# A SwiGLU block's down projection in Strassen form: evictions, refill pieces and row transfers moved to other steps

## The reference, cut to what matters

```python
h = _rms_norm(x, norm_ffn[l])
g = h @ w_gate[l].astype(h.dtype)
u = h @ w_up[l].astype(h.dtype)
x = x + (jax.nn.silu(g) * u) @ w_down[l].astype(h.dtype)
```

## Time and profile before

| | us |
|---|---|
| median of 3 runs | 2599.43 (2596.59 to 2600.51) |
| the profiled execution's own time | 2598.14 |
| its span, first to last instruction | 2596.4 |
| PE busy | 2463.3 (95% of the span) |
| DVE, ACT, POOL busy | 1414.1, 1165.6, 1311.5 |
| mean granted TensorE clock | 0.984 of full speed |

### The profile page before, as it was taken

The page is one execution under the profiler, slowest core; times in us unless marked ns, Lnnn a source line. Parts: engine busy times, 40 slices in busy tenths (PEclk is TensorE's granted clock), DMA queues, the critical chain, the costliest instruction groups (busy, mean ns, idle before and its releaser), DMA issues.

```text
span 2596.4 us, 34828 instructions
## 1 busy us (share of the span) xinstructions
PE 2463.3 (95%) x12008; PEld 2032.5 (78%) x12008; DVE 1414.1 (54%) x1463; ACT 1165.6 (45%) x1864; POOL 1311.5 (51%) x916
## 2 busy tenths in 40 slices
PE   8899999999899999799979999999999999999999
PEld 6777877777777777678768888888777888888887
DVE  4333366776676666533665555553645555553343
ACT  3222267676677676432343333324443333332433
POOL 1454366767667677300465445422785544551243
PEclk9999999999999999899989999999999999999999
DMA  5988863443443432254323332348663233224766
GB/s 178 302 264 279 258 182 100 135 107 94 128 107 97 143 90 68 75 173 138 146 89 113 112 119 75 109 170 294 206 205 126 73 109 121 87 99 159 228 216 203
DMA packets 337225, 388.17 MB, mean 150 GB/s; under 512 B 21440, under 2 KB 242752, under 8 KB 334784
## 3 DMA queue, kind: packets, MB, share of 16 engines
q1 hardware_dynamic: 337088, 386.49, 46.9%
HBM read 263.20 MB, written 123.21 MB: 149 GB/s over the span
## 4 chain that ended last, share of the span: by engine, by line
PE 44%; POOL 3%; DMA 1%; DVE 1%; issue 1%; ACT 0%; SPq 0%; DVEq 0%; POOLq 0%; ACTq 0%
PE ffn_ps L2184 10%; PE ffn_ps L2186 10%; PE ffn_ps L2188 10%; PE ffn_ps L2214 4%; PE ffn_ps L2216 4%; PE ffn_ps L2215 4%; POOL ffn_A L2103 1%; DMA ffn_raw<-in_w_up 1%; POOL ffn_A L2108 1%; POOL all_B L2130 0%; DMA ffn_A_over<-in_w_down 0%; ACT ffn_A L1796 0%; DMA ffn_A_over<-x 0%; POOL ffn_s L2114 0%; DVE ffn_A L1975 0%
## 5 line engine op out<-in xcount | busy, mean ns | idle before, releaser
L2103 POOL TENSOR_TENSOR ffn_A<-ffn_raw,ffn_A 128x512 fp32r<-128x512 f32 x264 | 366.1, 1399 | 381.3 <-ACT ffn_A L1754 381.3
L2184 PE MATMUL ffn_ps<-all_B,ffn_A 128*128 128x512 f32 x1232 | 482.1, 391 | 17.8 <-POOL ffn_A L2103 15.3
L2186 PE MATMUL ffn_ps<-all_B,ffn_A 128*128 128x512 f32 x1232 | 481.5, 391 | 0.0
L2188 PE MATMUL ffn_ps<-all_B,ffn_A 128*128 128x512 f32 x1232 | 481.3, 391 | 0.0
L1059 DVE TENSOR_TENSOR_SCAN lay_stick<-lay_ps,lay_stick 128x128 f32<-128x128 f32 (+5 forms) x192 | 331.2, 1726 | 199.5 <-ACT lay_ps L963 189.6
L1110 POOL TENSOR_TENSOR lay_a<-lay_a,lay_stick 128x128 f32<-128x128 f32 (+5 forms) x192 | 281.4, 1472 | 219.9 <-DVE lay_stick L1059 219.1
L1754 ACT ACTIVATE ffn_A<-ffn_raw 128x512 fp32r<-128x512 f32 x264 | 162.2, 626 | 291.0 <-DMA ffn_raw<-in_w_gate 122.8
L2184 PEld LDWEIGHTS ffn_ps<-all_B,ffn_A 128*128 128x128 f32 x1232 | 232.5, 189 | 67.5 <-POOL ffn_A L2103 19.0
L1796 ACT ACTIVATE ffn_A<-ffn_A_over 128x1024 fp32r<-128x1024 f32 x154 | 163.1, 1060 | 253.0 <-PE ffn_ps L2216 227.7
L1975 DVE TENSOR_TENSOR ffn_A<-ffn_A_over,ffn_A 128x1024 fp32r<-128x1024 f32 x104 | 154.5, 1489 | 212.9 <-ACT ffn_A L1796 212.9
L2188 PEld LDWEIGHTS ffn_ps<-all_B,ffn_A 128*128 128x128 f32 x1232 | 232.4, 189 | 48.3
(11 more groups left out here) (135 smaller groups left out, 5036.0 us busy)
## 6 DMA issues: line engine op xcount, KB each, us to landing
hid_ops<-ffn_s SPq DMA_DIRECT2D x154, 256.0 KB, 2.0
ffn_A_over<-hid_ops SPq DMA_DIRECT2D x154, 256.0 KB, 3.0
lay_w_stage<-in_w_in SPq DMA_DIRECT2D x48, 512.0 KB, 4.2
ffn_raw<-in_w_gate SPq DMA_DIRECT2D x22, 1024.0 KB, 5.4
ffn_raw<-in_w_up SPq DMA_DIRECT2D x22, 1024.0 KB, 7.6
ffn_A_over<-wd_ops SPq DMA_DIRECT2D x88, 256.0 KB, 3.5
ffn_A_over<-in_w_down SPq DMA_DIRECT2D x66, 256.0 KB, 3.9
lay_wd_raw<-in_w_down SPq DMA_DIRECT2D x11, 1024.0 KB, 8.5
```

The lines of the kernel that those rows point to most:

```text
L2103: nc.gpsimd.tensor_tensor(A[:, j, p, 1, :, :], operand(j, p), A[:, j, p, 0, :, :].bitcast(F32), ALU.subtract).then_inc(lo_done, 1)
L2184: nc.tensor.matmul(ps[:, b, :], A[:, j, p, 0, k, :], B[p][:, 0, k, :], start=first_mm, stop=False, skip_group_check=True)
L2186: nc.tensor.matmul(ps[:, b, :], A[:, j, p, 0, k, :], B[p][:, 1, k, :], start=False, stop=False, skip_group_check=True)
L2188: mm = nc.tensor.matmul(ps[:, b, :], A[:, j, p, 1, k, :], B[p][:, 0, k, :], start=False, stop=last_mm, skip_group_check=True)
```

## The change

On DVE the evictions after D2, D7 and D4 are spread, one bank a step behind the step's low part (steps 24 to 27, 46 to 49, 58 to 61), where before all four stood in one step ahead of it (24, 46, 57). Those after D6 and D5 stay. The refill begins earlier: two `load_b` a step in steps 10 to 17 (one a step in 10 to 25), combinations from step 20 (26), high parts from 25 (31), low parts from 29 (34), a little farther apart. `y_to_21` begins at step 50 (51). `store_z` 0 and 1 stand at steps 34 and 67 (31 and 64), `load_z` 1 and 3 at 36 and 69 (34 and 67); `load_z` 2 stays at 53. The raw places are given to other products' tiles, so that round 11's `hi` of products 2 to 5 wait for single low parts. That of product 2 is issued ahead of the last `split`, and those of products 8 to 13 between the round's `keep`s; round 12's first two come behind them.

```diff
--- before.py
+++ after.py
@@ -1494,7 +1494,7 @@
 SUMS = [(GATE, P5), (GATE, P7), (UP, P5), (UP, P7), (GATE, P6), (UP, P6), (GATE, P3), (UP, P3)]
 C11, C12, C22, C21 = range(4)
 D1, D2, D6, D7, D4, D5, D3 = range(7)
-T_AT, B_HI_AT, B_LO_AT = 26, 31, 34
+T_AT, B_HI_AT, B_LO_AT = 20, 25, 29
 
 
 def ffn_stage(nc, cst, B, Bf, offset, x2_dram, h2_dram, ops_dram, wt_dram, w_gate, w_up, w_down, out):
@@ -1560,14 +1560,15 @@
 
             return of[:, j, p, :, :, :].rearrange("p h k c -> p (h k c)")
 
-        op_raw = [flat(Af, j, p) for j, p in ((GATE, P5), (GATE, P6), (UP, P5), (UP, P6))]
+        op_raw = [flat(Af, j, p) for j, p in ((UP, P6), (GATE, P5), (GATE, P6), (UP, P5))]
         hi_of = [flat(A, j, p) for j, p in ((GATE, P7), (UP, P7), (UP, P2))]
         lo_of = [flat(A, j, p) for j, p in ((GATE, P2), (GATE, P4), (UP, P4))]
         hid_part, wd_part = slice(0, BANK), slice(BANK, 2 * BANK)
         SETS = ((6, 7, 2, 3), (0, 1, 4, 5))
         set_of = {D1: 0, D2: 0, D6: 1, D7: 1, D4: 0, D5: 1, D3: 1}
 
-        hi_at, lo_at = ([first + 7 * m // 5 for m in range(28)] for first in (B_HI_AT, B_LO_AT))
+        hi_at, lo_at = ([first + 10 * m // 7 for m in range(28)] for first in (B_HI_AT, B_LO_AT))
+        t_at = [T_AT + 4 * m // 3 for m in range(16)]
 
         def z_pair(i):
 
@@ -1631,7 +1632,7 @@
             def load_op(G, e):
                 R, (d, c) = last_round(G), divmod(e, ROUNDS)
                 if e < RAWS:
-                    sp.wait_ge(prod_done, NP * R + 1 + (spot[GATE, P5], spot[GATE, P6], spot[UP, P5], spot[UP, P6])[e])
+                    sp.wait_ge(prod_done, NP * R + 1 + (spot[UP, P6], spot[GATE, P5], spot[GATE, P6], spot[UP, P5])[e])
                 else:
                     wait_lo(sp, G, e - RAWS)
                 if e == 0:
@@ -1716,17 +1717,18 @@
                     load_op(G, e)
                     if e == 9:
                         load_z(G, 0)
-                    if G == 0 and e - 10 in range(4 * GT):
-                        load_b(e - 10)
-                    if e == ENDS[D2] + 10:
+                    if G == 0 and e - 10 in range(2 * GT):
+                        load_b(2 * (e - 10))
+                        load_b(2 * (e - 10) + 1)
+                    if e == ENDS[D2] + 13:
                         store_z(G, 0)
-                    if e == ENDS[D2] + 13:
+                    if e == ENDS[D2] + 15:
                         load_z(G, 1)
                     if e == 53:
                         load_z(G, 2)
-                    if e == ENDS[D4] + 10:
+                    if e == ENDS[D4] + 13:
                         store_z(G, 1)
-                    if e == ENDS[D4] + 13:
+                    if e == ENDS[D4] + 15:
                         load_z(G, 3)
                 store_z(G, 2)
                 store_w(G)
@@ -1745,8 +1747,11 @@
                 if R and R % ROUNDS == 0:
                     G = R // ROUNDS
                     if p in (P5, P6):
-                        act.wait_ge(dve_lo, ON_DVE * G)
-                        act.wait_ge(pool_lo, ON_POOL * G)
+                        wait_lo(act, G - 1, STEPS - RAWS + ((GATE, P5), (GATE, P6), (UP, P5), (UP, P6)).index((j, p)))
+                    elif (j, p) in ((UP, P2), (UP, P4)):
+                        act.wait_ge(tile_done, GT * (STEPS * G - 2))
+                    elif (j, p) in ((GATE, P7), (GATE, P2)):
+                        act.wait_ge(tile_done, GT * (STEPS * G - 1))
                     elif p in (P7, P2, P4):
                         act.wait_ge(tile_done, GT * STEPS * G)
                     elif p == P3:
@@ -1864,10 +1869,20 @@
                     more = R + 1 < HALVES * ROUNDS
                     ahead = more and not last
                     keep(R, GATE, 0)
+                    if c == 0:
+                        hi(R, 8)
+                        hi(R, 9)
                     keep(R, UP, 0)
-                    if more:
+                    if c == 0:
+                        hi(R, 10)
+                        hi(R, 11)
+                    if more and c:
                         hi(R + 1, 0)
                     keep(R, GATE, 1)
+                    if c == 0:
+                        hi(R, 12)
+                        hi(R, 13)
+                        hi(R + 1, 0)
                     if more:
                         hi(R + 1, 1)
                     if ahead:
@@ -1906,8 +1921,10 @@
                     split(G, e)
                     if G == 0 and e in hi_at:
                         b_hi_piece(hi_at.index(e))
+                    if e == STEPS - 2 and G + 1 < HALVES:
+                        hi(ROUNDS * (G + 1), 2)
                 if G + 1 < HALVES:
-                    for n in range(2, NP):
+                    for n in range(3, 8):
                         hi(ROUNDS * (G + 1), n)
 
         @block.vector
@@ -2081,14 +2098,17 @@
                     hidden(R, 3)
                     sums_of_hidden(R)
                 for e in range(OPS, STEPS):
-                    for d, evict in ((D2, evict_11), (D6, evict_w), (D7, evict_y), (D4, evict_21), (D5, evict_22)):
+                    for d, evict in ((D6, evict_w), (D5, evict_22)):
                         if e == ENDS[d] + OPS:
                             for t in range(GT):
                                 evict(G, t)
                     if e % 3 < 2:
                         op_lo(G, e)
-                    if G == 0 and e - T_AT in range(16):
-                        t_piece(e - T_AT)
+                    for d, evict, after in ((D2, evict_11, 3), (D7, evict_y, 3), (D4, evict_21, 4)):
+                        if e - ENDS[d] - after in range(GT):
+                            evict(G, e - ENDS[d] - after)
+                    if G == 0 and e in t_at:
+                        t_piece(t_at.index(e))
                 for t in range(GT):
                     evict_12(G, t)
                 if G + 1 < HALVES:
@@ -2142,7 +2162,7 @@
                 for e in range(STEPS):
                     if e % 3 == 2:
                         op_lo(G, e)
-                    for at, add in ((39, x2_to_w), (51, y_to_21), (ENDS[D5] + 4, y_to_22)):
+                    for at, add in ((39, x2_to_w), (50, y_to_21), (ENDS[D5] + 4, y_to_22)):
                         if e - at in range(0, 2 * GT, 2):
                             add(G, (e - at) // 2)
                     if G == 0 and e in lo_at:
```

## The result

| | before | after |
|---|---|---|
| median us (4 runs each) | 2598.01 (2596.51 to 2600.51) | 2616.72 (2614.34 to 2618.87) |
| profiled execution, us | 2598.14 | 2618.87 |
| span, us; mean granted clock | 2596.4; 0.984 | 2617.1; 0.982 |

The ratio is 1.0071, with a 95% interval of 1.0053 to 1.0088: the change makes the kernel 0.7% slower. PE's work is the same; what grew is the time in which it waits, and the time at the lower clock behind the waits.

A forecast was written before the change was run, and what follows sets the result against it. PE was taken as the bound, with some 13 us to gain from a better order of the first half. The terms summed to +13.3 on 2598.1, giving 2611 us, range 2600 to 2618.

The forecast's parts named there:

- crowded transfers: Rival: transfers of steps 10 to 17 become a bound, PE stalls repeatedly with a slow clock; 2617 us, chance 0.12.
- step 33: First half, at `evict_w`: one more POOL piece in the way of DVE, +1.1 us (0 to 1.3).
- step 11 (loads of B crowded): Steps 10 to 17: two blocks of B a step leave a lag, `keep_x` behind a late `split`; +0.5 us (0 to 3).
- steps 42 and 44: First half: two DVE combinations and one POOL piece less, waits shrink; -3.5 us (-4.2 to -2.5).
- step 53: First half: POOL's low part late behind the addition waiting for z, two pieces and a second addition; +4.7 us (1 to 7).
- steps 56 and 57: First half: additions done earlier and `evict_21` begins at 58, so both waits and their slow clock go; -3.8 us.
- step 66, first half: `evict_22` waits for the later fourth load of z, itself held by the store; +5.0 us, with the clock +6.6.
- round 11: The 2.49 wait goes, but round 12's weights load later: 2.5 idle at product 8, 1.5 at 9; +1.5 us (0 to 2.5).
- step 66, second half: Same late load of z, as SP's queue is one code for both halves; +4.6 us, with the clock +6.2.
- The clock: Behind a long wait PE runs at the lower clock, costing 1.6 us; a wait soon after another costs 1.2 to 1.6.
- the clock would hold: Rival: no slow clock behind the long waits and step 53 on time; 2602 us, chance 0.18.
- the load of z is hidden: Rival: the fourth load of z lands before DVE reaches `evict_22`, and step 53 is on time; 2594 us, chance 0.07.

The follow-up runs named there:

- experiment 6: Changed kernel with the refill's high and low parts back at steps 31 and 34, old spacing; combinations and loads stay early: 2612.55 us, ratio 1.0052.
- experiment 7: Changed kernel with the four `evict_w` moved ahead of step 34's combination: 2613.72 us, ratio 1.0057.
- experiment 3: Changed kernel with `y_to_21` beginning at step 51 again, as before: 2614.09 us, ratio 1.0058.
- experiment 4: On top of experiment 1, the third load of z at SP's step 50 instead of 53: 2596.10 us, ratio 0.9993.
- experiment 1: Changed kernel with the second store and fourth load of z back at SP's steps 64 and 67: 2603.83 us, ratio 1.0017.
- experiment 2: Kernel before with only the second store and fourth load of z moved to SP's steps 67 and 69: 2611.89 us, ratio 1.0053.
- experiment 8: On top of experiment 1, `keep` of products 5 and 8 ahead of round 12's `hi`: 2600.88 us, ratio 1.0009.
- experiment 5: Changed kernel with the refill's whole schedule (loads, combinations, high and low parts) back as before: 2610.45 us, ratio 1.0041.

## Why the prediction was right, and where its sizes were off

It said 2611 (2600 to 2618), slower; measured is 2616.7. The direction and the largest mechanism were right, and the sum is 5 to 6 short of it. That the time lies within the range is partly luck: the sum itself was expected at 2606 to 2614, and the range went up to 2618 for crowded transfers, which cost 0.8 here. What fills that room is above all step 33. Idle time and slow stretches by place, after minus before:

| place | predicted | measured |
|---|---|---|
| step 11 (loads of B crowded) | +0.5 | +0.8 |
| step 33 | +1.1 | +6.4 |
| steps 42 and 44 | -3.5 | -4.3 |
| step 53 | +4.7 | +6.9 |
| steps 56 and 57 | -3.8 | -4.0 |
| step 66, first half | +6.6 | +7.2 |
| round 11 | +1.5 | 0.0 |
| step 66, second half | +6.2 | +6.5 |
| sum | +13.3 | +19.5 |

The sum is 0.6 above the 18.9 that the profiled execution is longer by from step 0 on: the slow stretches are counted from starts of matmuls, and each is good to some tenths.

*Step 33* is the term that failed. "That puts one more piece in the way: +1.1 (0 to 1.3)" counted one of POOL's instructions and one turn. The order of DVE's list is unchanged there, as it said. But it left out the three pieces of steps 29 to 31. From the first of them on seven of the eight DVE instructions ahead of `evict_w`, all on two SBUF operands, take 1.8 to 2.9 us where they take 0.7 or 1.2 alone, and by the time of step 34's combination POOL's low part of step 35 has begun: another whole 2.44. Experiments 6 and 7 show both parts: without the early pieces 1.05, without that combination ahead 2.23 for 4.97. A wait of 5 us then also pays the clock, 2.5 here, which a wait of 1.04 had not.

By the Trainium skill, SBUF — State Buffer, section SBUF: two separate sides, DVE and POOL share a pair of ports to SBUF under an exclusive lock, which a DVE instruction with two inputs in SBUF needs as well. The rows of step 33 agree: a combination of 2.83 beside a POOL instruction of 2.44, and of 0.68 where POOL is idle. The four evictions, which read one operand from PSUM, take 2.47 beside POOL as before, as the prediction took from the page.

*Steps 42, 44, 56, 57:* right in place and within 0.8 of size. The reason given for 44 was half wrong: by experiment 6 it is POOL's pieces at their new steps, and the two combinations fewer on DVE do little there. With the additions back at 51 (experiment 3) 0.85 is at step 56 and nothing at 57, which speaks for the moved `evict_21` at 57; it was not tried alone.

*Step 53:* the mechanism was right (experiments 3 and 4). PE arrives there later than assumed, by the wait at step 33, and so does SP's load, by about as much (2.9 and 2.7 us after step 0). The idle time came out at 4.66 and the slow stretch at 2.3, for 3.1 and 1.6: from z to the low part's end it took 9.4, for the 8.5 of the prediction's working, and from the load's issue to the first addition 7.8 for 7.1.

*Step 66:* the size of the idle time was right to within 0.8: 5.05 for 5.8 (5.0 and the 0.80 of before) and 5.60 for 5.0 (4.6 and the 0.44). Experiments 1 and 2 show the mechanism from both sides. But one term of its working was too large: it let the store land 6.7 after its issue, so that it held the load of z by 1.3 in the first half and by 0.5 in the second. The store took 5.3 and 6.0, and the load follows step 69's loads at once. The load's second transfer in turn took 7.3 and 7.9 instead of the 7.0 assumed. These errors have opposite signs, and over the two halves they cancelled, which is luck. The cause is the load's two places later in SP's queue; in experiment 3 the store's landing adds 1.0 to it.

The Trainium skill's fit that the prediction sets beside this (DMA: Bandwidth & Descriptors, Anatomy of one DMA) is given there for transfers that GpSimd issues, and here SP does. By it the waits would have been some 3 us shorter; they were not.

*Round 11:* the mechanism was right (experiment 8), the size not. The second weights came 6.5 after their issue, not the 7.7 taken from the earlier trace rows, so the waits are 1.23 and 1.25. Timeline of SP and ACT, after:

```profile
1986.50 0.38 SPq L1617 DMA_DIRECT2D ffn_raw<-in_w_up  x1
1993.02 0.63 ACT L1759 ACTIVATE ffn_A<-ffn_raw 128x512 fp32r<-128x512 f32 x1 [2.06 <-DMA ffn_raw<-in_w_up]
1994.08 0.58 ACT L1779 ACTIVATE ffn_s<-ffn_ps 128x512 f32<-128x512 f32 x1
```

*The clock:* 1.6 behind a long wait was too little. It was 2.3 and 2.9 in the first half and 1.3 in the second, 6.5 for 4.8 over the three places where it was forecast, beside the 2.5 at step 33 that was not.

*The rivals:* that the clock would hold is excluded, 0.50 behind each of the first half's three long waits; that the load of z is hidden is excluded by DVE's idle 4.17 and 5.07 until its landing; the crowded transfers cost 0.84, at one place (at most 1.3 there in the other kernels that keep them). The spread evictions were not tried alone. Nor was it tried what moving the first store and second load of z (34 and 36) does by itself; no wait stands there.

## What to carry to other kernels

Find for each transfer the instruction that waits for it, and compare the time from its issue to that with the longest landing in the trace, not the median: two places later in a full queue cost 13 us here, because one order is run in both halves. Where DVE and POOL both read their operands from SBUF, a short instruction ahead of an eviction can cost as much as POOL's longest one, so what frees a PSUM bank belongs ahead of all that may have to take a turn. Before a small difference is explained, look at the stretches that the change cannot touch: here step 0 begins at 1731.3 to 1740.0 in the eleven profiled executions, 8.7 us apart, though PE's work ahead of it is the same in all.

## What the runs showed of the hardware that was not expected

The granted clock after a wait does not follow from its length, nor from a smaller wait ahead of it. A wait of 1.80 at step 57 was followed by a slow stretch in the kernel before, and the same one, 1.78 long behind 0.56, by none in experiment 2. It stayed at 1.00 behind waits of 2.49, 2.81 (experiment 5), and 2.03 in experiment 6:

```profile
1856.70:1860.70 4.00, 4.00 (x18) 3.31 (x19) 2.13 (x3) 0.99 (x2) 4.00 (x3) 1.00 0.59 191
```

A wait of 1.85 at the turn in experiment 4, alone in its surroundings, cost 1.35 more. From step 0 on, the clock fell behind every wait of 3.07 or more in these runs. So between 1.8 and 3 us the price was either nothing or 1.3 to 1.7, and what decides it stays open; the prediction's rule, that a wait soon after another is the one that costs, is refuted.

The load of z did not land equally fast in the same place of the queue: the waits that it sets at step 66 lie between 5.0 and 6.4 us in the kernels with the late load, and single loads of z take 4.8 to 8.5 over all runs. What makes the difference was not tried.
